# The squared-ReLU MLP of a two-layer decoder step: eight buffers for streamed operands, token groups of 3, 2 and 3, and token operands prepared operand by operand

## The reference, cut to what matters

```python
def rmsnorm(x, g):
    x32 = x.astype(F32)
    y = x32 * lax.rsqrt(jnp.mean(x32 * x32, axis=-1, keepdims=True) + NORM_EPS) * g.astype(F32)
    return y.astype(x.dtype)

def sq_relu_mlp(xn, w1, w2):
    return jnp.square(jax.nn.relu(xn @ w1)) @ w2

# in the loop over the layers, g = norm_g[l]:
xp = xp + rmsnorm(sq_relu_mlp(rmsnorm(xp, g[4]), w_ff1[l], w_ff2[l]), g[5])   # 1024 x 1024
xs = xs + rmsnorm(sq_relu_mlp(rmsnorm(xs, g[4]), w_ff1[l], w_ff2[l]), g[5])   # 32 x 1024
```

## Time and profile before

| | |
|---|---|
| median of 3 runs | 3717.67 us (3717.34 to 3720.66) |
| the profiled execution, its own time | 3724.84 us |
| its span, first to last instruction | 3723.0 us |
| mean granted TensorE clock | 0.940 |
| TensorE busy | 3300.7 us (89%) |
| VectorE busy | 1864.7 us (50%) |
| ScalarE busy | 1420.7 us (38%) |

### The profile page before, as it was taken

One profiled execution on the slowest core, in us unless ns is written; L12 is line 12 of the kernel. 1 busy time (PEld: TensorE's weight loads), 2 busy tenths in 40 slices (PEclk: granted clock), 3 DMA queues, 4 the chain that ended last, 5 costly groups with the idle time before them and its releaser, 6 DMA issues. The chain is left out here.

```text
span 3723.0 us, 43104 instructions
## 1 busy us (share of the span) xinstructions
PE 3300.7 (89%) x16243; PEld 2429.1 (65%) x16243; DVE 1864.7 (50%) x3389; ACT 1420.7 (38%) x2593; POOL 156.2 (4%) x168
## 2 busy tenths in 40 slices
PE   8879988877988999999967999988888999999975
PEld 6724643455775777788744777676776777788743
DVE  5667996533435755544423341075435655544422
ACT  6454644632435422234422431263436322234422
POOL 0020110041000000000000000011000000000000
PEclk9989998998999999999988999998998999999987
DMA  3122112074122232375432111102122223375433
GB/s 102 25 69 77 40 49 100 13 247 160 35 91 85 79 106 91 115 242 173 138 112 75 60 35 35 35 6 74 35 91 85 94 91 102 128 228 174 141 105 112
DMA packets 212145, 358.66 MB, mean 96 GB/s; under 512 B 40807, under 2 KB 128591, under 8 KB 211940
## 3 DMA queue, kind: packets, MB, share of 16 engines
q1 hardware_dynamic: 200164, 313.96, 26.4%
q0 software_dynamic: 11776, 41.95, 3.4%
HBM read 303.42 MB, written 52.13 MB: 96 GB/s over the span
## 5 line engine op out<-in xcount | busy, mean ns | idle before, releaser
L179 PE MATMUL ps<-s_mlp_w2l,s_mlp_hh 128*128 128x512 f32 x1024 | 425.5, 415 | 111.5 <-DVE s_mlp_hl L873 107.3
L868 DVE TENSOR_TENSOR s_mlp_w2l<-s_mlp_w2b,s_mlp_w2h 128x1024 fp32r<-128x1024 f32 x192 | 235.2, 1225 | 544.1 <-ACT s_mlp_w2h L705 544.1
L705 ACT CAST s_mlp_w2h<-s_mlp_w2b 128x1024 fp32r<-128x1024 f32 x192 | 201.5, 1049 | 605.2 <-PE ps L181 311.2
L181 PE MATMUL ps<-s_mlp_w2h,s_mlp_hh 128*128 128x512 f32 x1024 | 419.1, 409 | 0.0
L180 PE MATMUL ps<-s_mlp_w2h,s_mlp_hl 128*128 128x512 f32 x1024 | 418.0, 408 | 0.0
L179 PE MATMUL ps<-s_mlp_XB,s_mlp_W 128*128 128x512 f32 x896 | 364.9, 407 | 12.1 <-DVE s_mlp_W L840 12.1
L181 PE MATMUL ps<-s_mlp_XB,s_mlp_W 128*128 128x512 f32 x896 | 356.2, 398 | 0.0
L180 PE MATMUL ps<-s_mlp_XB,s_mlp_W 128*128 128x512 f32 x896 | 353.9, 395 | 0.0
L179 PEld LDWEIGHTS ps<-s_mlp_w2l,s_mlp_hh 128*128 128x128 f32 x1024 | 203.2, 198 | 194.9 <-DVE s_mlp_w2l L868 121.9
L181 PEld LDWEIGHTS ps<-s_mlp_w2h,s_mlp_hh 128*128 128x128 f32 x1024 | 203.4, 199 | 45.2
L180 PEld LDWEIGHTS ps<-s_mlp_w2h,s_mlp_hl 128*128 128x128 f32 x1024 | 204.2, 199 | 41.8
(11 more groups left out here) (590 smaller groups left out, 6253.4 us busy)
## 6 DMA issues: line engine op xcount, KB each, us to landing
s_mlp_w2b<-w_ff SPq DMA_DIRECT2D x192, 512.0 KB, 4.0
s_mlp_raw<-w_ff SPq DMA_DIRECT2D x32, 1024.0 KB, 5.9
hidden_scratch<-x SPq DMA_DIRECT2D x128, 256.0 KB, 2.0
s_mlp_hraw<-hidden_scratch SPq DMA_DIRECT2D x128, 192.0 KB, 3.1
x_kb<-cache_mem_k SPq DMA_DIRECT2D x16, 512.0 KB, 7.5
x_vb<-cache_mem_v SPq DMA_DIRECT2D x2, 4096.0 KB, 20.6
x_scratch<-x SPq DMA_DIRECT2D x16, 512.0 KB, 2.6
x<-x_scratch SPq DMA_DIRECT2D x16, 512.0 KB, 4.3
```

Source lines behind the costliest of these rows:

```text
L179: nc.tensor.matmul(out, ah, bl, start=first, stop=False, skip_group_check=True)
L181: return nc.tensor.matmul(out, ah, bh, start=False, stop=last, skip_group_check=True)
L705: nc.scalar.copy(w2h[:, s % 3], w2b[:, s % 4]).then_inc(high2, 1)
L868: nc.vector.tensor_tensor(w2l[:, s % 3], w2b[:, s % 4], w2h.bitcast(F32)[:, s % 3], ALU.subtract).then_inc(low2, 1)
```

## The change

There are three parts, all in `stage_mlp`. The rings `w2b` and `hraw` get eight buffers (`AHEAD`). The groups become tiles (0, 1, 2), (3, 4) and (5, 6, 7). The token operands of the first product are prepared in the order of the operands: B11 of all four slices first, then slices 2 and 3 of all others, then slices 0 and 1 operand by operand; there are four scratch buffers `full` (two lie in memory of `W` that is used later), and product 0 is issued in the midst of the transposes. Since `w2b` is larger, it lies on other parts of `XB`, and several waits and the places of loads change with it. The diff, cut:

```diff
-    low_at = {B11: 0, B21: 1, B22: 2, T1: 3, T3: 4, T2: 5, T4: 6}
-    order_x = (B11, B21, B22, T1, T3, T2, T4)
-    groups = [(0, 3), (3, 3), (6, 2)]
+    turns = [(0, k) for k in (2, 3, 0, 1)] + [(q, k) for k in (2, 3, 0, 1) for q in (1, 3, 2)]
+    operands = ([(B11, k) for k in (2, 3, 0, 1)] + [(o, k) for k in (2, 3) for o in (B22, T1, T3, B21, T2, T4)]
+                + [(o, k) for o in (B21, B22, T2, T1, T3) for k in (0, 1)] + [(T4, 1), (T4, 0)])
+    groups = [(0, 3), (3, 2), (5, 3)]
+    AHEAD = 8
-    tail_at = {NF * (g + 1) - 1 + i: 3 * g + i for g in range(2) for i in range(3)}
+    tail_at = {NF * (g + 1) - 1 + i: groups[g][0] + i for g in range(2) for i in range(groups[g][1])}
+    reload_at = {8: 0, 10: 1, 12: 2, 20: 3, 22: 4, 72: 5, 74: 6, 76: 7}
...
             def load_w2(s):
                 f = s % NF
-                if s < 4:
+                if s < AHEAD:
+                    sp.wait_ge(product, N - (5 if s < 3 else 4 if s < 7 else 3))
+                else:
+                    sp.wait_ge(low2, s - AHEAD + 1)
+                if s - AHEAD >= 2 * NF:
+                    sp.wait_ge(sample_used, (s - AHEAD - 2 * NF) // 2 + 1)
+                sp.dma_start(w2b[:, s % AHEAD], w2v[:, f, :]).then_inc(w2_in[s % AHEAD], 16)
...
                     if p == PAIRS - 1 and j == 0:
-                        for s in range(4):
+                        for s in range(2):
+                            load_h(s)
                             load_w2(s)
+                    if p == PAIRS - 1 and j == 1:
+                        for s in range(2, 4):
                             load_h(s)
+                            load_w2(s)
...
-            sp.dma_start(gB[:], bc(gain.rearrange("(o n) -> o n", o=1), [P, D])).then_inc(gain_row_in, 16)
             for s in range(4, S_ALL):
                 load_w2(s)
                 load_h(s)
-                if s % 2 == 0 and s < 20:
-                    t = s // 2 - 2
+                if s == AHEAD:
+                    sp.wait_ge(product, N)
+                    sp.dma_start(gB[:], bc(gain.rearrange("(o n) -> o n", o=1), [P, D])).then_inc(gain_row_in, 16)
+                if s in reload_at:
+                    t = reload_at[s]
                     sp.dma_start(G.x[:, t, :], G.xd[:, t, :]).then_inc(x_in[t], 16)
...
+            for e in range(7):
+                turn(e)
+            pe.wait_ge(scaled_act, 3)
             for k in range(KD):
                 ins = nc.tensor.transpose(G.ps[:, 7, k * NS:(k + 1) * NS], s_scaled[:, k * P:(k + 1) * P], G.ident[0:NS, 0:NS])
             ins.then_inc(s_turned, 1)
+            for e in range(7, 10):
+                turn(e)
+            multiply(0)
+            for e in range(10, 16):
+                turn(e)
+                warm(2)
+            warm(16)
...
@@ scalar: before, gain_x of a slice, then round_x of a slice; after: @@
+            for t in (2, 3):
+                nc.scalar.activation(G.x[:, t, :], G.x[:, t, :], ACT.Copy, scale=stat[:, t:t + 1]).then_inc(scaled_act, 1)
+            for k in (2, 3, 0, 1):
+                gain_x(0, k)
+            for k in (2, 3, 0, 1):
+                round_x(B11, k)
+            round_w(0)
...
@@ vector: @@
+            for t in (0, 1, 4, 5, 6, 7):
                 nc.vector.tensor_scalar(G.x[:, t, :], G.x[:, t, :], stat[:, t:t + 1], None, ALU.mult).then_inc(scaled_dve, 1)
+            for k in (2, 3, 0, 1):
+                low_x(B11, k)
+            low_w(0)
+            for k in (2, 3):
+                sum_x(T1, k)
+                sum_x(T3, k)
+                low_x(B22, k)
+                sum_x(T2, k)
+                for o in (T1, T3, B21):
+                    low_x(o, k)
+                sum_x(T4, k)
+                for o in (T2, T4):
+                    low_x(o, k)
             dve.wait_ge(s_turned, 1)
+            nc.vector.tensor_tensor(xs[:], ...)
+            low_w(1)
+            for k in (0, 1):
+                low_x(B21, k)
+            for k in (0, 1):
+                sum_x(T1, k)
+                sum_x(T3, k)
+                low_x(B22, k)
+                sum_x(T2, k)
             sum_w(1)
             sum_w(2)
+            for k in (0, 1):
+                low_x(T2, k)
+            low_w(2)
...
             def low_w2(s):
+                if s == 0:
+                    dve.wait_ge(product, N - 2)
                 dve.wait_ge(high2, s + 1)
...
-            tail(6)
-            tail(7)
-            tail(8)
-            for t in range(6, 9):
+            for t in range(5, 9):
+                tail(t)
+            for t in range(5, 9):
                 square_x(t)
```

More of the change, by code:

```diff
@@ L408, in stage_mlp @@
         rs = S.sb("rs", [P, NT + 1])
+        xs = S.sb("xs", [P, KD, NS])
         first = ExitStack()
@@ L473, in tile_bank, with gains_to, ready, summed_to @@
             return 2 * ((t + 1) % 4)
+        def gains_to(q, k):
+            return turns.index((q, k)) + 1
+        def ready(o, k):
+            return operands.index((o, k)) + 1
+        def summed_to(o, k):
+            return differences.index((o, k)) + 1
         @block.sync
@@ L485, in load_w2, with load_h @@
                 f = s % NF
-                if s < 4:
+                if s < AHEAD:
[5 more added lines that the diff above has]
+                sp.dma_start(w2b[:, s % AHEAD], w2v[:, f, :]).then_inc(w2_in[s % AHEAD], 16)
+            def load_h(s):
+                g, f = steps[s]
+                if s < AHEAD:
                     sp.wait_ge(product, N - 6)
                 else:
[L489 to L499, removed]
+                    sp.wait_ge(low_h, s - AHEAD + 1)
                 t0, n = groups[g]
-                sp.dma_start(hraw[:, s % 4, 0:n * P], G.hd[f, :, t0 * P:(t0 + n) * P]).then_inc(h_in[s % 4], 16)
+                sp.dma_start(hraw[:, s % AHEAD, 0:n * P], G.hd[f, :, t0 * P:(t0 + n) * P]).then_inc(h_in[s % AHEAD], 16)
             for p in range(PAIRS):
@@ L564, in multiply @@
                     pe.wait_ge(gained, 16)
+                if p == 0:
+                    pe.wait_ge(x_low, max(ready(i, k) for k in range(4)))
                 a = 5 * p + (0, 1, 0, 2, 3, 4, 3)[i] - 7
@@ L621, in down_sample, with turn @@
                         o = 64 * q + 32 * n
-                        ins = nc.tensor.matmul(G.ps[o:o + NS, 2, :], hs[:, s % NF - 1 + q, :], w2b[:, (s - 1 + q) % 4, n * 512:(n + 1) * 512],
+                        ins = nc.tensor.matmul(G.ps[o:o + NS, 2, :], hs[:, s % NF - 1 + q, :], w2b[:, (s - 1 + q) % AHEAD, n * 512:(n + 1) * 512],
                                                start=(s == 2 * NF + 1), stop=(s == S_ALL - 1), tile_position=(0, o))
                 ins.then_inc(sample_used, 1)
-            pe.wait_ge(scaled_act, 1)
+            def turn(e):
+                q, k = turns[e]
+                kk, half = k + 4 * (q // 2), q % 2
+                if e >= 5:
+                    pe.wait_ge(gained, e - 4)
+                for j in range(4):
+                    if e == 0 and j == 0:
+                        pe.wait_ge(scaled_dve, 2)
+                    if e == 0 and j >= 2:
+                        pe.wait_ge(scaled_act, j - 1)
+                    if e == 4:
+                        pe.wait_ge(scaled_dve, j + 3)
+                    ins = nc.tensor.transpose(G.ps[:, 1 + e % 5, j * P:(j + 1) * P], G.x[:, 4 * half + j, kk * P:(kk + 1) * P], G.ident[:])
+                ins.then_inc(turned, 1)
+            for e in range(7):
+                turn(e)
+            pe.wait_ge(scaled_act, 3)
             for k in range(KD):
@@ L660, in used_before @@
             if f == 0:
-                eng.wait_ge(tile_done, 3 * g)
+                eng.wait_ge(tile_done, groups[g][0])
             else:
@@ L666, in _, with gain_x @@
         def _(act):
-            def gain_x(e):
-                k, quarter = divmod(e, 4)
-                kk = k + 4 * (quarter // 2)
+            def gain_x(q, k):
+                e, kk = turns.index((q, k)), k + 4 * (q // 2)
                 if e == 0:
@@ L928, in _ @@
+            for k in (0, 1):
+                low_x(T1, k)
+            low_w(3)
+            sum_w(4)
+            for k in (1, 0):
+                sum_x(T4, k)
+            for k in (0, 1):
+                low_x(T3, k)
+            low_w(4)
             sum_w(5)
-            for m in range(3, LEAD):
-                low_w(m)
+            low_w(5)
+            for k in (1, 0):
+                low_x(T4, k)
             for n in range(N + 2):
@@ L958, in _ @@
                     dve.wait_ge(s_rectified, p + 1)
+                    if p == 0:
+                        dve.wait_ge(x_low, len(operands))
                     nc.vector.tensor_tensor(hs[:, 2 * p:2 * p + 2, :], stmp, stmp, ALU.mult).then_inc(s_squared, 1)
```

172 lines of the change are left out of this document (82 added, 90 removed).

## The result

The changed kernel takes 3596.91 us (median of 4 runs, 3594.36 to 3597.03) against 3719.11 us before (median of 4): a ratio of 0.967, 95% interval 0.9653 to 0.9687. The forecast was 3552 us, 3530 to 3590. The direction was right; the saving was 122 us, not the 167 forecast. In the profiled executions the span fell from 3723.0 to 3595.1 us.

The account below looks back on a forecast made before the run. Third groups were taken to wait for w2 loads held behind sample products, other groups bound by TensorE. Terms -83.1 - 77.2 + 3.7 - 12.0 + 2.6 = -166.0 gave 3558.8 us profiled, 3552 forecast as median, range 3530 to 3590.

Parts of the forecast that it names:

- The step that failed: Preparation in each MLP: product 2, read as released by a low part of W, starts earlier; -6.0 us, bounds -11 and 0.
- the walk: Preparation: ScalarE's and VectorE's lists followed against each other, with some 6 us of waits, to product 2 at 2900.6.
- What follows on TensorE is the same: Preparation: after product 2 TensorE's work is unchanged, so its -6.0 us carries through in each MLP.
- First group: First token group, second product: later store and loads make step 1 wait some 3.2 us; +2.3 and +1.4 us.
- Middle group: Second token group, now two tiles: buffers' order forces a pitch of 2.85 us; -38.6 us in each MLP.
- The tile ends: Middle group's first three steps: three tile ends of the group before add 3.0 us beyond the 2.85 pitch.
- Last group: Third token group, now three tiles: w2 loads leave the chain, two steps at about 9.25 us; -43.5 and -39.6 us.
- change of stream: Last group: each of 16 sample products costs 1.04 us plus one such change, 1.1 together; 16.5 us counted.
- End: After the last matmul: one more prompt tile is normalised; +1.3 us in each MLP.
- the one of casts: Rival, two-tile steps: casts bind them at a pitch of 3.21 us; +23 us, 3575; chance 0.08.
- the one of transfers: Rival, two-tile steps: transfer rate of 168 GB/s binds, a step takes 3.90 us; +67 us, 3619; chance 0.04.
- Preparation gives nothing: Rival, preparation: VectorE's queue stays as long and waits in other places; +12 us, 3564; chance 0.05.

Follow-up runs that it names:

- e_u1: Changed kernel with ScalarE's copy `u1` of product 0 issued right behind the rounding of the second weight operand; 3585.5 us, ratio 0.9631 to 0.9664.
- e_gt: Changed kernel with the load of the gain column issued ahead of the 1 MB of weights; 3591.7 us, ratio 0.9647 to 0.9680.
- e_fix: e_part and e_gt together, plus the loads of steps 2 and 3 put back behind the first store; 3568.4 us, ratio 0.9578 to 0.9604.
- e_part: e_u1 with ScalarE's copies `u2` and `part` also moved up, behind the rounding of weight operand 8; 3580.8 us, ratio 0.9621 to 0.9648.
- e_rings: e_fixdve with rounded weights in four buffers instead of three and rounded hidden rows in three instead of two; 3549.8 us, ratio 0.9533 to 0.9565.
- e_fixdve: e_fix with two of VectorE's pair 0 combinations moved ahead of low parts 9 and 10; 3561.1 us, ratio 0.9566 to 0.9592.

## Why the prediction was wrong, and where it was right

**The step that failed** is the preparation's: product 2 "released by a low part of W". Its -6.0 became +6.4 and +5.8, outside its bounds of -11 and 0. The prediction took the releaser that a row named and walked only ScalarE's roundings and VectorE's list from there. Product 2 also waits for `u1_kept`, and the walk left out where that copy stands. In the old order it came 0.1 us before product 2; in the new one it stands behind roundings that were put last on purpose. The error in mlp0 is 12.4 us: 9.4 is the copy's (product 2 in e_u1), 2.1 the load of the gain column (product 2 in e_gt), which was not waited for while ScalarE scaled four tiles first and is now that it scales two; 1.0 lies between products 2 and 7, since product 2 now runs wholly at the low clock. The walk itself was sound to 0.1 or 0.2: with the gain column first the first rounding comes 6.96 us into the stage (1200.80 - 1193.84 in e_gt), 6.97 by the prediction, and with both gone product 2 comes at 38.6 (e_fix), against 38.8.

"What follows on TensorE is the same" held nearly where product 2 was late (18.4 us to product 7 before, 19.4 after), but not once it was early: then `part`, and then VectorE's combinations, were late next (e_u1, e_part). The prediction named neither.

**First group:** mechanism right, size too small. The store and the order of ScalarE's roundings gave a wait of 3.88 us, 3.2 forecast (the terms named for it add up to 3249.5, not 3249.8, so to 2.9); the load's 5.0 us in place of 3.65 make up for that. The term left out is the low clock behind it, 2.4 us in step 1 of mlp1. The prediction put the stall in as lost time and let the engine come back at full speed.

**Middle group:** 2.91 against the 2.85 that was argued from the buffers' order. e_rings shows that order to be the cause. The tile ends were sized right: the first three steps take 3.41, 4.12 and 4.12 us in mlp1, 3.1 us beyond 2.85 each, 3.0 forecast. The rest of the miss is the pitch, 0.06 x 29 = 1.7; steps alternate between 2.84 and 2.99, and no run shows why every second one is longer.

**Last group:** two steps at 9.39 us instead of 9.25 (4.22 and 5.17), 16 x 0.14 = 2.2 us: all of the miss. The prediction counted one change of stream for each sample product; the change back costs too. The first matmul behind the product is followed after 0.34 us (3435.26 to 3435.60), not 0.23.

**End:** right, +1.3.

**The rivals:** the one of casts (pitch 3.21) and the one of transfers fell: the middle group moves 218 and 219 GB/s, e_rings 225 at a pitch of 2.72. The Trainium skill, "Perfetto Trace Analysis", section "DMA Optimizations", holds that transfers under 2 KB cost a significant overhead each. If a row of a load counts as a transfer, no run here shows that price: loads of 128 KB in rows of 1024 bytes took 3.2 us to land in mlp1's middle group, those of 192 KB in rows of 1536 bytes 3.8, and neither bound anything. The 2.3 of the earlier trace rows is of four loads only; 28 of the same size in mlp1's third group took 4.3 (median) in the kernel before. "Preparation gives nothing" came nearest, but it looked for the waits in VectorE's queue; the wait was in ScalarE's, and the sign worse than that rival allowed.

e_fixdve comes to 3561.1 us, near the forecast, but partly by luck, since errors cancel: in each MLP its preparation is the forecast's, its first group 3.3 us better (130.6 for 133.9), its middle and last groups together some 4 us worse.

Between the two profiled executions, 3724.84 and 3596.95 us, lie 127.9 us, between the medians 122.2: the one before was above its median, the one after on it.

## What to carry to other kernels

When a list is reordered, write down every semaphore that the consumer waits for and find each producer's new place in its engine's own list; a releaser that a profile names is only the last of several, and sometimes not even that. An engine's order is a promise to everyone who waits on it, so what is small and awaited (a copy that frees a bank, a column of gains) goes ahead of what is long and not yet needed. Buffers that take a load off a chain pay whatever the order of the groups (70 to 76 us in each second product); the order without the buffers paid 12 to 14.

## What the runs showed of the hardware that was not expected

The clock after a pause is not told by the pause's length alone. In e_u1 TensorE idled 3.48 us ahead of product 2 and ran it at 1.00 (2.4 GHz), and 3.25 us ahead of the fold and ran product 5 at 0.50 (1.2 GHz); in e_fixdve 4.17 us (mlp1) was followed by 0.50. That start, and the stretch behind it (length, PE busy, clock, DMA share, GB/s):

```profile
2812.99 0.79 PE L179 MATMUL ps<-s_mlp_XB,s_mlp_W 128*128 128x512 f32 x1 [4.17 <-DVE s_mlp_W L902]
```

```profile
2813.00:2816.00 3.00, 3.00 (x7) 0.50 0.00 0
```

In e_part (mlp0) product 2 came back at 1.00 after 3.58 us and the clock fell within it: 0.63 on the mean from 1231.7 to 1236.3. A start at 0.50 cost 2.4 us in product 2 (5.4 us to the next instruction in the changed kernel's mlp0, 3.0 in e_u1's) and 2.4 in a step of eighteen (6.50 for 4.08), beside the wait itself.

A gain column of 4 KB, issued 0.44 us behind a load of 1 MB, was waited for until 5.5 us after its issue (1191.19 to 1196.66); issued ahead of that load, it was there 3.9 us after it at the latest (1193.79 to 1197.71 in e_gt).
